# Seven block products in place of eight: Strassen's scheme in the second up projection of an fp32 encoder layer

## Chip, cores and metric

The kernel runs on one core of one Trainium2 chip. The metric is the device time of one execution in microseconds (us). A gap of 0.2% of it, 1.9 us, is about what a measurement of this kernel can tell from no change.

## What is computed

One encoder layer on 512 tokens of width 1024, all in float32, with three sub-layers: a SwiGLU feed-forward block (width 2816), a token mixer (latent attention beside causal pooling), and a second SwiGLU block. The change touches the second block:

```python
def _swiglu(h, w_in, w_out):
    g, u = jnp.split(h @ w_in, 2, axis=-1)
    return (jax.nn.silu(g) * u) @ w_out

h = x * (1.0 + scale[:, 2, None, :]) + shift[:, 2, None, :]
y = _swiglu(h, ffn2_w_in[l], ffn2_w_out[l])
x = _layernorm(ALPHA * x + 0.5 * gate[:, 2, None, :] * y, post_ln_g[l, 2], post_ln_b[l, 2])
```

## The kernel before, in words

Everything lies transposed: features on the 128 partitions, 512 tokens in the free direction. `h` is 8 tiles of 128x512 (KD = 8), the hidden layer is 22 tiles (FT = 22). Each float32 product is made of three passes in the type fp32r: an operand is split into a rounded part (`hi`) and the rest (`lo`), and `mm3` (L599 to L601) issues hi by hi, hi by lo and lo by hi. So one weight unit of 128x1024 (eight 128x128 blocks) costs 24 matmuls of 512 columns.

The weights come as a stream of units. SyncE loads a unit into one of 3 buffers `raw` (L521), ScalarE rounds it to `w_hi` (`act_hi`, L1054), VectorE subtracts and leaves `w_lo` (`dve_lo`, L1082), TensorE uses it; `w_hi` and `w_lo` have 4 slots. The order on each engine is written out by hand and held together by semaphores that count steps (`s_hi`, `s_lo`, `s_used`).

In the up stage of a feed-forward block each hidden tile t has a pair of units, gate and up. Into two PSUM banks go 24 matmuls each. Then ScalarE takes Silu of the gate bank (L1189), VectorE multiplies by the up bank (L1577), ScalarE rounds the product to `a_hi` (L1180), GpSimd leaves the rest in `a_lo` (L1926). In the down stage that follows, each of 8 output tiles takes three units (8, 8 and 6 blocks, 66 matmuls), and VectorE adds the result to the residual stream `x` (L1565). The last output tile is done in two halves of 256 tokens, 66 matmuls each of 256 columns, so that the closing LayerNorm overlaps it. During this tail only matmuls of 256 columns are to be seen.

The second block begins behind the LayerNorm of the mixer. Its first three units run on an un-normalised `h` (`opening`), the fourth and the pairs t = 2 to 21 are plain (`up`). GpSimd makes `h_lo` and scales `x` for the residual (L1920) before it comes to its first `a_lo`.

Of the kernel before, what the change touches and what calls it, by code (L numbers as in the profile page):

```python
# [22 lines left out]
P = 128  # L23
# [60 lines left out]
LAST_K = FT - 8 * (DPM - 1)  # L84

# [87 lines left out]
def source(n, wunits):  # L173
# [12 lines left out]
    return wunits[n][:, 0:unit_width(n)]  # L186
# [7 lines left out]
def unit_width(n):  # L194

    for down, end in ((F1_DOWN, MX), (F2_DOWN, UNITS)):
        if down <= n < end and (n - down) % DPM == DPM - 1:
            return LAST_K * P
    return UNIT


def build(nc, xT, wunits, ada_w, c_rows, pos_rows, cols_dram, pool_w, outT):
# [4 lines left out]
    with ExitStack() as ctx:  # L207
# [29 lines left out]
        rstd = sb("rstd", [P, TOK])
# [16 lines left out]
        ident = cols[:, C_ID:C_ID + P]  # L254

# [79 lines left out]
        def x_pair(group, half):  # L335
            return x[:, group[0]:group[1] + 1, tokens(half)]
# [17 lines left out]

        def wg(n):
# [12 lines left out]
        s_x = [sem(f"x_loaded{i}") for i in range(X_LOADS)]  # L368
        s_ada1 = [sem(f"ada_first_loaded{i}") for i in range(FIRST_RING)]
# [76 lines left out]
        s_x0 = sem("tile0_rounded")  # L446
        tile0 = {1: h_hi[:, 2, :], 2: lat[:, 2 * KD - 1, :], 3: h_hi[:, 2, :]}
# [57 lines left out]
        def _(sp):  # L505
# [197 lines left out]

# [1412 lines left out]
```

## Time and profile before

| | us |
|---|---|
| three timed runs, median (lowest to highest) | 951.12 (950.44 to 951.27) |
| profiled execution, first to last instruction (span) | 949.2 |
| TensorE busy in the span | 937.3 (99%) |
| VectorE, ScalarE, GpSimd busy | 505.9, 374.3, 267.7 |

The page gives the profiled execution by its span alone; its own time has no other figure, and the span lies 1.9 us below the median of the timed runs. PE is TensorE, PEld its weight loads, DVE VectorE, ACT ScalarE, POOL GpSimd and SP SyncE. An instruction's duration reaches from its start to the end of its last write, and on PE, DVE and ACT the next one starts before that end. So a rate is read from one start to the next, and a duration tells when a waiting engine can go on.

### The profile page before, as it was taken

How to read it: one execution, taken by the hardware profiler on the slowest of the kernel's cores; microseconds unless marked ns; L12 is line 12 of the kernel's file. 1: busy time of each engine (PE TensorE's matmuls, PEld its weight loads, DVE VectorE, ACT ScalarE, POOL GpSimd, SP SyncE). 2: the span in 40 equal slices, each digit the busy share in tenths (PEclk: the TensorE clock that was granted, in tenths of full speed). 3: DMA queues.
4: the chain of work that ended last, by engine and by line, in shares of the span. 5: the costliest groups of instructions: out<-in, count | busy, mean ns of one | idle time of the engine just before them, and what ended most of it. 6: DMA issues, size and time to landing. Idle time of an engine off the chain costs nothing.

```text
span 949.2 us, 10888 instructions
## 1 busy us (share of the span) xinstructions
PE 937.3 (99%) x4233; PEld 757.8 (80%) x4233; DVE 505.9 (53%) x714; ACT 374.3 (39%) x567; POOL 267.7 (28%) x222
## 2 busy tenths in 40 slices
PE   8999999999999999999999999999999999999997
PEld 5788888888888888788767687788888888888886
DVE  6956767545454865677666488532322322233334
ACT  6752232242222223574496457533223223221224
POOL 0021111111104512346854585611111111135125
PEclk9999999999999999999999999999999999999999
DMA  9936565656644662222421121333232232223402
GB/s 357 369 125 208 180 204 193 193 171 214 195 155 140 235 233 93 83 84 104 133 68 45 45 76 59 121 105 106 89 109 92 89 108 86 84 68 116 121 19 89
DMA packets 38563, 127.21 MB, mean 134 GB/s; under 512 B 4080, under 2 KB 6256, under 8 KB 38512
## 3 DMA queue, kind: packets, MB, share of 16 engines
q1 hardware_dynamic: 37968, 126.00, 39.5%
q8 instruction: 33, 0.54, 0.2%
q10 hardware_dynamic: 544, 0.52, 0.2%
q14 instruction: 18, 0.15, 0.0%
HBM read 123.36 MB, written 2.10 MB: 132 GB/s over the span
## 4 chain that ended last, share of the span: by engine, by line
PE 93%; DVE 3%; ACT 2%; DMA 1%; SPq 1%; issue 0%; POOL 0%; ACTq 0%; DVEq 0%
PE bank L599 29%; PE bank L601 29%; PE bank L600 29%; PE bank L957 2%; PE bank L981 1%; DMA ada_first<-ada_w 1%; PE bank L968 1%; PE bank L684 1%; PE bank L685 1%; DVE w_lo L1082 1%; PE bank L678 1%; SPq L509 0%; PE bank L874 0%; ACT act_t L1135 0%; PE bank L725 0%
## 5 line engine op out<-in xcount | busy, mean ns | idle before, releaser
L1082 DVE TENSOR_TENSOR w_lo<-raw,w_hi 128x1024 fp32r<-128x1024 f32 x152 | 204.1, 1350 | 277.7 <-ACT w_hi L1054 277.3
L599 PE MATMUL bank<-h_hi,w_hi 128*128 128x512 f32 x727 | 284.6, 391 | 0.1
L601 PE MATMUL bank<-h_hi,w_lo 128*128 128x512 f32 x727 | 283.0, 389 | 0.0
L600 PE MATMUL bank<-h_lo,w_hi 128*128 128x512 f32 x727 | 282.9, 389 | 0.0
L1054 ACT ACTIVATE w_hi<-raw 128x1024 fp32r<-128x1024 f32 x153 | 155.8, 1031 | 189.8 <-PE bank L601 188.5
L1926 POOL TENSOR_TENSOR a_lo<-act_t,a_hi 128x512 fp32r<-128x512 f32 x44 | 59.0, 1340 | 420.2 <-ACT a_hi L1180 420.2
L599 PEld LDWEIGHTS bank<-h_hi,w_hi 128*128 128x128 f32 x727 | 136.5, 188 | 29.0 <-DVE w_lo L1082 0.6
L601 PEld LDWEIGHTS bank<-h_hi,w_lo 128*128 128x128 f32 x727 | 136.4, 188 | 28.7
L600 PEld LDWEIGHTS bank<-h_lo,w_hi 128*128 128x128 f32 x727 | 136.5, 188 | 27.7
L599 PE MATMUL bank<-a_hi,w_hi 128*128 128x512 f32 (+1 forms) x374 | 141.2, 377 | 0.0
L600 PE MATMUL bank<-a_lo,w_hi 128*128 128x512 f32 (+1 forms) x374 | 140.8, 377 | 0.0
L601 PE MATMUL bank<-a_hi,w_lo 128*128 128x512 f32 (+1 forms) x374 | 140.8, 377 | 0.0
L599 PEld LDWEIGHTS bank<-a_hi,w_hi 128*128 128x128 f32 x374 | 70.4, 188 | 13.0
L600 PEld LDWEIGHTS bank<-a_lo,w_hi 128*128 128x128 f32 x374 | 70.4, 188 | 13.0
L601 PEld LDWEIGHTS bank<-a_hi,w_lo 128*128 128x128 f32 x374 | 70.4, 188 | 12.8
L1421 DVE SCALAR_TENSOR_TENSOR var<-ada_ring,c_act 128x1024 bf16<-128x1024 f32 x56 | 72.5, 1295 | 3.0 <-DMA ada_ring<-ada_w 3.0
L1180 ACT ACTIVATE a_hi<-act_t 128x512 fp32r<-128x512 f32 x44 | 27.8, 632 | 107.6 <-DVE act_t L1577 104.8
L1944 POOL TENSOR_TENSOR s_sum<-s_sum,x 128x512 f32<-128x512 f32 x17 | 27.5, 1615 | 108.0 <-DVE x L1565 105.8
L1162 ACT ACTIVATE sq<-x 128x512 f32<-128x512 f32 x20 | 12.6, 632 | 105.9 <-DVE x L1565 96.8
L1565 DVE SCALAR_TENSOR_TENSOR x<-bank,gate,x 128x512 f32<-128x512 f32 x15 | 11.2, 749 | 63.6 <-PE bank L601 58.3
L1189 ACT ACTIVATE act_t<-bank 128x512 f32<-128x512 f32 x42 | 25.1, 597 | 43.0 <-PE bank L601 43.0
L1935 POOL TENSOR_TENSOR x<-x,shift 128x512 f32<-128x512 f32 x16 | 25.9, 1656 | 56.3 <-DVE shift L1562 56.3
(304 smaller groups left out, 1046.7 us busy)
## 6 DMA issues: line engine op xcount, KB each, us to landing
raw<-wunits SPq DMA_DIRECT2D x145, 512.0 KB, 3.3
ada_ring<-ada_w SPq DMA_DIRECT2D x56, 512.0 KB, 4.4
ada_first<-ada_w SPq DMA_DIRECT2D x16, 512.0 KB, 11.4
raw<-wunits SPq DMA_DIRECT2D x16, 384.0 KB, 2.9
x<-xT SPq DMA_DIRECT2D x8, 256.0 KB, 4.9
outT<-x SPq DMA_DIRECT2D x6, 256.0 KB, 2.7
K<-k_rope SPq DMA_DIRECT2D x2, 512.0 KB, 7.8
c_act<-c_rows SPq DMA_DIRECT2D x1, 512.0 KB, 6.1
```

The lines of the kernel that those rows point to most:

```text
L599: mm(out, lh, rh, start=first, stop=False)
L600: mm(out, lh, rl, start=False, stop=False)
L601: return mm(out, ll, rh, start=False, stop=last)
L957: mm(bank[S_BANK[k % 2]][:, 0:(i + 1) * P], Q[:, hd % QRING, i * P:(i + 1) * P], K[:, hd, 0:(i + 1) * P], start=True, stop=True).then_inc( ...
L1054: nc.scalar.activation(parts(n, 0, width)[0], raw[:, slot, 0:width], ACT.Copy)\
L1082: nc.vector.tensor_tensor(lo, raw[:, slot, 0:width], hi.bitcast(F32), SUB).then_inc(s_lo, 1)
L1180: fn(a_hi[:, t - 1, :], act_t[:, (t - 1) % 2, :], ACT.Copy).then_inc(s_ah[f], 1)
L1189: fn(act_t[:, t % 2, :], bank[up_bank(f, t)][:], ACT.Silu).then_inc(s_silu[f], 1)
L1421: stt(junk, slot_ap, 1.0, c_act[:], MUL, MUL, accum_out=mod[:, t:t + 1])\
L1926: tt(a_lo[:, t, :], act_t[:, t % 2, :], a_hi[:, t, :].bitcast(F32), SUB)\
L1935: tt(x[:, m, :], x[:, m, :], shift[:], SUB).then_inc(s_xs[p], 1)
L1944: tt(s_sum[:], s_sum[:], x[:, m, :], ADD).then_inc(s_acc[p], 1)
```

## The change

For the pairs t = 5 to 21 (17 of 22) the gate and the up tile are taken together as a 2x2 scheme. The rows of blocks are gate and up, the inner dimension is halved (4 blocks of `h` each) and the tokens are halved (256 each). Plain multiplication needs eight products of 128x512 by 512x256. Winograd's form of Strassen's scheme needs seven, p1 to p7, each of 4 blocks by 3 passes, 12 matmuls of 256 columns (L984 to L986), and adds sums:

- Four sums of `h` (`t_raw`, 128x4x256 each), once, on DVE (`combine_h`), each rounded by ACT and its rest taken by DVE.
- Four sums of weight blocks for each pair. Two (up first + up second half, gate first + up first half) are made by DMA: SP loads one addend, GpSimd issues a DMA with `accum_op=ADD` that adds the other from DRAM (`add_block`). Two (`s2`, `s4`) are made by DVE, 128x512 each (`weight_sums`).
- Per pair ACT rounds 128x1024 three times and 128x512 once, and DVE takes as many rests (`rest`), where before both had two of 128x1024.
- Seven sums of results. PSUM accumulation takes two; ACT copies p1 out (`first_copy`) and DVE does five of 128x256 (`u2`, `u3`, `ub`, `ua`, `gb`). Silu is taken in two halves. One multiplication of 128x512 on DVE ends the pair.

p4 and p3 of pair t are put between p6 and p5 of pair t+1. The buffers take the room of the weight slots, in two sets; the rests are written over the raw weights. For room, `x` goes to DRAM (2 stores of 1 MB) when the stage begins, and comes back as `x2` after p4 of the last pair (4 loads of 512 KB). ACT no longer waits for `h_lo` while it makes `h` in this sub-layer, since the whole `h` is kept in `h_full`. The first five units of the down stage have waits of their own. Nothing changes before the LayerNorm of the second block.

```diff
+T0 = 5
...
+def product_order():
+    out = []
+    for t in range(T0, FT + 1):
+        if t < FT:
+            out += [("p1", t), ("p6", t)]
+        if t > T0:
+            out += [("p4", t - 1), ("p3", t - 1)]
+        if t < FT:
+            out += [("p5", t), ("p2", t), ("p7", t)]
+    return out
...
+            def load_c(t):
+                if t == T0:
+                    sp.wait_ge(s_lo, D2 - 2)
+                elif t == T0 + 1:
+                    sp.wait_ge(s_used, D2)
+                else:
+                    sp.wait_ge(s_blk, PRODUCT["p5", t - 2])
+                sp.dma_start(raw_13[in_set(t)][:, 0:BLOCK], up_unit(t)[:, 0:BLOCK]).then_inc(s_cl[in_set(t)], 16)
...
+            load_c(T0)
+            load_ab(T0)
+            load_a3(T0)
+            load_d(T0)
+            sp.wait_ge(s_res[2], KD)
+            for half in range(2):
+                k = slice(KH * half, KH * (half + 1))
+                sp.dma_start(spill[k].rearrange("t p n -> p t n"), x[:, k, :]).then_inc(s_spill, 16)
+            load_ab(T0 + 1)
+            load_c(T0 + 1)
+            load_a3(T0 + 1)
+            for t in range(T0 + 2, FT):
+                load_c(t)
+                load_ab(t)
+                load_a3(t)
+                load_d(t - 1)
+            unit(D2)
+            unit(D2 + 1)
+            load_d(FT - 1)
+            for n in range(D2 + 2, D2 + LEAD + 2):
+                unit(n)
+            sp.wait_ge(s_blk, PRODUCT["p4", FT - 1])
+            sp.wait_ge(s_spill, LOADED + 32)
+            for i in range(4):
+                sp.dma_start(x2[:, 2 * i:2 * i + 2, :], spill[2 * i:2 * i + 2].rearrange("t p n -> p t n"))\
+                    .then_inc(s_x2[i], 16)
+            for n in range(D2 + LEAD + 2, STREAM):
                 unit(n)
...
+            def product(kind, t, out, first, last):
+                hi, lo = block_parts(kind, t)
+                for kk in range(KH):
+                    cols = slice(kk * P, (kk + 1) * P)
+                    high, low = moving(kind, kk)
+                    nc.tensor.matmul(out[:, 0:HALF], hi[:, cols], high, start=first and kk == 0, stop=False, skip_group_check=True)
+                    nc.tensor.matmul(out[:, 0:HALF], hi[:, cols], low, start=False, stop=False, skip_group_check=True)
+                    done = nc.tensor.matmul(out[:, 0:HALF], lo[:, cols], high, start=False, stop=last and kk == KH - 1,
+                                            skip_group_check=True)
+                done.then_inc(s_blk, 1)
+            def block_products():
+                for t in range(T0, FT + 1):
+                    if t < FT:
+                        first, second, third = pair_banks(t)
+                        pe.wait_ge(s_blo, REST["ab", t])
+                        if t < T0 + 2:
+                            pe.wait_ge(s_prod[1], t - 1)
+                        else:
+                            pe.wait_ge(s_gs, SILU["a", t - 2])
+                        product("p1", t, first, True, True)
+                        pe.wait_ge(s_blo, REST["2", t])
+                        if t >= T0 + 2:
+                            pe.wait_ge(s_bsum, SUM["ua", t - 2])
+                        product("p6", t, second, True, True)
+                    if t > T0:
+                        _, before, gated = pair_banks(t - 1)
+                        pe.wait_ge(s_blo, REST["d4", t - 1])
+                        pe.wait_ge(s_bsum, SUM["u3", t - 1])
+                        product("p4", t - 1, before, False, True)
+                        pe.wait_ge(s_bsum, SUM["ub", t - 1])
+                        product("p3", t - 1, gated, False, True)
+                    if t < FT:
+                        pe.wait_ge(s_blo, REST["13", t])
+                        if t >= T0 + 2:
+                            pe.wait_ge(s_bsum, SUM["gb", t - 2])
+                        product("p5", t, third, True, True)
+                        pe.wait_ge(s_p1c, KD + t - T0 + 1)
+                        product("p2", t, first, False, True)
+                        pe.wait_ge(s_bsum, SUM["u2", t])
+                        product("p7", t, second, False, True)
...
+            def weight_sums(t):
+                s = in_set(t)
+                dve.wait_ge(s_acc1[s], added(t))
+                dve.wait_ge(s_ab[s], landed(t))
+                if t >= T0 + 2:
+                    dve.wait_ge(s_blk, PRODUCT["p6", t - 2])
+                sum_done(tt(raw_2[:, s, :], raw_13[s][:, 0:BLOCK], raw_ab[s][:, 0:BLOCK], ADD), "s2", t)
+                dve.wait_ge(s_bsum, SUM["s2", t])
+                if t >= T0 + 2:
+                    dve.wait_ge(s_blk, PRODUCT["p3", t - 2])
+                at = 2 * BLOCK * s
+                sum_done(tt(raw_d4[:, at:at + BLOCK], raw_2[:, s, :], raw_ab[s][:, BLOCK:2 * BLOCK], ADD), "s4", t)
+            def third_sums(t):
+                _, second, third = pair_banks(t)
+                dve.wait_ge(s_blk, PRODUCT["p7", t])
+                dve.wait_ge(s_p1c, KD + t - T0 + 1)
+                dve.wait_ge(s_prod[1], t)
+                sum_done(tt(up_sum[:, tokens(1)], p1_copy[:, in_set(t), :], second[:, 0:HALF], ADD), "u3", t)
+                dve.wait_ge(s_bsum, SUM["u3", t])
+                sum_done(tt(up_sum[:, tokens(1)], up_sum[:, tokens(1)], third[:, 0:HALF], ADD), "ub", t)
+            def second_sum(t):
+                dve.wait_ge(s_blk, PRODUCT["p6", t])
+                dve.wait_ge(s_p1c, KD + t - T0 + 1)
+                sum_done(tt(u2_sum[:, in_set(t), :], p1_copy[:, in_set(t), :], pair_banks(t)[1][:, 0:HALF], ADD), "u2", t)
...
+            def block_stage():
+                weight_sums(T0)
+                rest("ab", T0)
+                rest("2", T0)
+                product(F2, 1, T0 - 1)
+                for t in range(T0, FT + 1):
+                    if t > T0:
+                        third_sums(t - 1)
+                        rest("d4", t - 1)
+                    if t < FT:
+                        second_sum(t)
+                        rest("13", t)
+                    if t > T0:
+                        up_first(t - 1)
+                    if t + 1 < FT:
+                        weight_sums(t + 1)
+                    if t > T0:
+                        gate_second(t - 1)
+                    if t + 1 < FT:
+                        rest("ab", t + 1)
+                        rest("2", t + 1)
+                    elif t < FT:
+                        dve_lo(dve, D2)
+                        dve_lo(dve, D2 + 1)
+                    if t > T0:
+                        block_product(t - 1)
+                dve_lo(dve, D2 + 2)
...
+            def add_block(t, which):
+                s = in_set(t)
+                if which == 1:
+                    pool.wait_ge(s_cl[s], landed(t))
+                    pool.dma_start(raw_13[s][:, 0:BLOCK], wunits[F2 + 2 * t + 1][:, BLOCK:2 * BLOCK], accum_op=ADD)\
+                        .then_inc(s_acc1[s], 16)
+                else:
+                    pool.wait_ge(s_a3[s], landed(t))
+                    pool.dma_start(raw_13[s][:, BLOCK:2 * BLOCK], wunits[F2 + 2 * t + 1][:, 0:BLOCK], accum_op=ADD)\
+                        .then_inc(s_acc3[s], 16)
+            def ffn(f, p):
+                for t in range(FT if f == 0 else T0 - 2):
+                    a_split(f, t)
+                if f == 1:
+                    add_block(T0, 1)
+                    add_block(T0, 3)
+                    for t in range(T0, FT):
+                        if t + 1 < FT:
+                            add_block(t + 1, 1)
+                        a_split(f, t - 2)
+                        if t + 1 < FT:
+                            add_block(t + 1, 3)
+                    a_split(f, FT - 2)
+                    a_split(f, FT - 1)
```

**Order on VectorE.** Before, one pair of the second up stage (`w_lo` is the rest of a weight unit, `act_t` the multiplication):

```order
L1082 TENSOR_TENSOR w_lo<-raw,w_hi 128x1024 x2
L1577 TENSOR_TENSOR act_t<-act_t,bank1 128x512
L1082 TENSOR_TENSOR w_lo<-raw,w_hi 128x1024 x2
L1577 TENSOR_TENSOR act_t<-act_t,bank3 128x512
```

Now, one pair of the block stage in full (`up_sum` and `u2_sum` are sums of results, `lo_...` the rests, `raw_2` and `raw_d4` the sums s2 and s4 of the next pair's weights):

```order
L2117 TENSOR_TENSOR up_sum<-p1_copy,bank1 128x256
L2119 TENSOR_TENSOR up_sum<-up_sum,bank2 128x256
L2095 TENSOR_TENSOR lo_d4<-raw_d4,hi_d4 128x1024
L2125 TENSOR_TENSOR u2_sum<-p1_copy,bank6 128x256
L2095 TENSOR_TENSOR lo_13_0<-raw_13_0,hi_13_0 128x1024
L2130 TENSOR_TENSOR up_sum<-p1_copy,bank1 128x256
L2104 TENSOR_TENSOR raw_2<-raw_13_1,raw_ab1 128x512
L2109 TENSOR_TENSOR raw_d4<-raw_2,raw_ab1 128x512
L2136 TENSOR_TENSOR act_t<-u2_sum,bank2 128x256
L2095 TENSOR_TENSOR lo_ab1<-raw_ab1,hi_ab1 128x1024
L2095 TENSOR_TENSOR lo_2<-raw_2,hi_2 128x512
L2144 SCALAR_TENSOR_TENSOR act_t<-up_sum,act_t 128x512
```

Three instructions a pair have become twelve, and the two results that p4 waits for come first.

**Order on GpSimd**, at the beginning of the block stage; before, there stood only the rows of `a_lo`, one a pair:

```order
L2505 DMA raw_13_0<-wunits 128x512
L2509 DMA raw_13_0<-wunits 128x512
L2505 DMA raw_13_1<-wunits 128x512
L2470 TENSOR_TENSOR a_lo2<-act_t,a_hi2 128x512
L2509 DMA raw_13_1<-wunits 128x512
L2505 DMA raw_13_0<-wunits 128x512
L2470 TENSOR_TENSOR a_lo2<-act_t,a_hi2 128x512
```

Each `a_lo` now stands between two adding DMAs.

## Rows read from the trace of the kernel before

**Rows 1.** The page: busy time, TensorE's clock, the chain that ended last by engine.
```profile
PE 937.3 (99%) x4233; PEld 757.8 (80%) x4233; DVE 505.9 (53%) x714; ACT 374.3 (39%) x567; POOL 267.7 (28%) x222
PEclk9999999999999999999999999999999999999999
PE 93%; DVE 3%; ACT 2%; DMA 1%; SPq 1%; issue 0%; POOL 0%; ACTq 0%; DVEq 0%
```

**Rows 2.** Busy time by stretches of the second block: pairs 2-4, 5-21, down, tail.
```profile
core 0: us, PE busy (x) PEld busy (x) DVE busy (x) ACT busy (x) POOL busy (x), PEclk, DMA share, GB/s
598.30:630.90 32.60, 32.60 (x145) 26.95 (x144) 16.00 (x19) 12.29 (x16) 12.14 (x12) 1.00 0.43 145
630.90:815.90 185.00, 185.00 (x818) 153.18 (x817) 51.56 (x51) 54.83 (x68) 22.04 (x17) 1.00 0.29 96
815.90:920.60 104.70, 104.70 (x463) 86.69 (x462) 35.13 (x28) 23.54 (x28) 27.43 (x19) 1.00 0.26 83
```

**Rows 3.** PE in order of time: start us, duration, what; 512, then 256 columns.
```profile
894.77 0.39 PE L599 MATMUL bank<-a_hi,w_hi 128*128 128x512 f32 x1
...
920.61 0.28 PE L599 MATMUL bank<-a_hi,w_hi 128*128 128x256 f32 x1
...
928.40 0.28 PE L601 MATMUL bank<-a_hi,w_lo 128*128 128x256 f32 x1
928.52 0.28 PE L783 MATMUL bank<-h_hi,ones_d 128*128 128x256 f32 x1
```

**Rows 4.** DVE in order of time, tail: sums of 256 columns, and starts behind PE.
```profile
928.72 0.48 DVE L1483 SCALAR_TENSOR_TENSOR x<-bank,gate,x 128x256 f32<-128x256 f32 x1 [3.72 <-PE bank L601]
931.84 0.43 DVE L1487 SCALAR_TENSOR_TENSOR bank<-bank,tmp 128x256 f32<-128x256 f32 x1 [2.63 <-PE bank L795]
932.18 1.28 DVE L1491 TENSOR_TENSOR x<-x,bank 128x512 f32<-128x512 f32 x2
933.38 0.42 DVE L1494 TENSOR_TENSOR bank<-bank,y 128x256 f32<-128x256 f32 x1
933.83 0.43 DVE L1496 SCALAR_TENSOR_TENSOR bank<-bank,y 128x256 f32<-128x256 f32 x1
```

**Rows 5.** DVE in order of time, one pair of the second up stage.
```profile
632.04 1.23 DVE L1082 TENSOR_TENSOR w_lo<-raw,w_hi 128x1024 fp32r<-128x1024 f32 x1 [3.79 <-ACT w_hi L1054]
633.18 0.68 DVE L1577 TENSOR_TENSOR act_t<-act_t,bank 128x512 f32<-128x512 f32 x1
637.90 1.23 DVE L1082 TENSOR_TENSOR w_lo<-raw,w_hi 128x1024 fp32r<-128x1024 f32 x1 [4.04 <-ACT w_hi L1054]
```

**Rows 6.** ACT by groups, shapes apart: rounding, copies of 256 columns, rounding `a_hi`.
```profile
L1054 ACT ACTIVATE w_hi<-raw 128x1024 fp32r<-128x1024 f32 x137 | 143.5, 1054 | 181.1 <-PE bank L601 179.8 <-DMA raw<-wunits 1.3
L1107 ACT ACTIVATE tmp<-bank 128x256 f32<-128x256 f32 x2 | 0.8, 384 | 1.0 <-PE bank L789 1.0
L1180 ACT ACTIVATE a_hi<-act_t 128x512 fp32r<-128x512 f32 x18 | 11.4, 632 | 35.2 <-DVE act_t L1577 32.5 <-DVE act_t L1573 2.7
```

**Rows 7.** POOL and DVE in order of time, behind the last pair: the two overlap.
```profile
817.35 1.29 POOL L1926 TENSOR_TENSOR a_lo<-act_t,a_hi 128x512 fp32r<-128x512 f32 x1 [7.37 <-ACT a_hi L1180]
...
818.25 1.47 DVE L1082 TENSOR_TENSOR w_lo<-raw,w_hi 128x1024 fp32r<-128x1024 f32 x1 [1.65 <-ACT w_hi L1054]
```

**Rows 8.** DMA issues: size each, median us from issue to landing.
```profile
raw<-wunits SPq DMA_DIRECT2D x145, 512.0 KB, 3.3
K<-k_rope SPq DMA_DIRECT2D x2, 512.0 KB, 7.8
poolw<-pool_w SPq DMA_DIRECT2D x1, 256.0 KB, 2.9
```

**Rows 9.** PEld's longest idle piece early in the program, and a clock row around it.
```profile
23.49 0.30 PEld L678 LDWEIGHTS bank<-h_lo,w_hi 128*128 128x128 f32 x2 [1.55 <-DVE h_lo L1719]
...
20.00:30.00 10.00, 7.52 (x32) 4.74 (x32) 9.93 (x18) 9.89 (x15) 0.00 (x0) 1.00 1.03 418
```

More of the change, by code:

```diff
@@ L194, in unit_width @@
 def unit_width(n):
-    for down, end in ((F1_DOWN, MX), (F2_DOWN, UNITS)):
+    for down, end in ((F1_DOWN, MX), (D2, STREAM)):
         if down <= n < end and (n - down) % DPM == DPM - 1:
@@ L446, in build, with added, landed @@
         s_x0 = sem("tile0_rounded")
+        s_gs, s_p1c = s_xna, s_tfree
+        s_acc1 = [sem(f"first_sum_added{i}") for i in range(2)]
+        s_acc3 = [sem(f"third_sum_added{i}") for i in range(2)]
+        s_ab, s_cl, s_a3 = s_ada1[4:6], s_ada1[6:8], s_ada1[8:10]
+        s_d, s_spill, s_x2 = s_x[0], s_x[1], s_x[2:6]
+        LOADED = 16
+        s_blk, s_bhi, s_blo, s_bsum = s_tp, s_fc, s_tok, s_xk
+        PRODUCT = counts(product_order(), KD)
+        ROUNDED = counts(rounding_order(), KD)
+        REST = counts(rest_order(), 2 * QB)
+        SUM = counts(sum_order(), QB)
+        SILU = counts(silu_order(), 2 * QB)
+        def added(t):
+            return 16 * ((t - T0) // 2 + 1)
+        def landed(t):
+            return LOADED + 16 * ((t - T0) // 2 + 1)
         tile0 = {1: h_hi[:, 2, :], 2: lat[:, 2 * KD - 1, :], 3: h_hi[:, 2, :]}
@@ L837, in down, with ffn @@
                     down_tile(base, per, p, rhs, k_last, m, ready)
-            def ffn(base, f, p, a_hi, a_lo):
+            def ffn(base, down_base, f, p):
                 if f == 0:
@@ L1176, in up, with silu_whole @@
+            def silu_whole(base, f, t):
+                act.wait_ge(s_used, base + 2 * t + 1)
+                if t >= 2:
+                    act.wait_ge(s_al[f], t - 1)
+                fn(act_t[:, t % 2, :], bank[up_bank(f, t)][:], ACT.Silu).then_inc(s_silu[f], 1)
+            def up(base, f):
+                for t in range(FT + 1 if f == 0 else T0 - 1):
                     if t < FT and split_next(base, 2 * t) is not None and (f == 0 or t >= 2):
@@ new lines, in rest @@
+            def rest(kind, t):
+                s = in_set(t)
+                dve.wait_ge(s_bhi, ROUNDED[kind, t])
+                if kind in ("ab", "2"):
+                    dve.wait_ge(s_bsum, SUM["s4", t])
+                if kind == "T":
+                    out, whole, hi = t_lo[:, t], t_raw[:, t], t_hi[:, t]
+                elif kind == "ab":
+                    out, whole, hi = lo_ab[s][:], raw_ab[s][:], hi_ab[s][:]
+                elif kind == "2":
+                    out, whole, hi = lo_2[:, s, :], raw_2[:, s, :], hi_2[:, s, :]
+                elif kind == "13":
+                    out, whole, hi = lo_13[s][:], raw_13[s][:], hi_13[s][:]
+                else:
+                    out, whole, hi = lo_d4[:, d4_columns(t)], raw_d4[:, d4_columns(t)], hi_d4[:]
+                tt(out, whole, hi.bitcast(F32), SUB).then_inc(s_blo, 1)
@@ L1642, in ffn @@
                     product(base, f, t)
-                for t in range(early, FT + 1):
+                for t in range(early, FT + 1 if f == 0 else T0 - 1):
                     for j in range(2):
-                        if t < FT and (f == 0 or 2 * t + j >= LEAD):
+                        if t < FT and (f == 0 or LEAD <= 2 * t + j < 2 * T0 - LEAD):
                             dve_lo(dve, split_next(base, 2 * t + j))
@@ L1652, in ffn @@
                         rope_chunk(t - ROPE_FIRST)
+                if f == 1:
+                    combine_h()
+                    for j in range(4):
+                        rest("T", j)
+                    product(base, f, T0 - 2)
+                    block_stage()
                 if f == 0:
```

454 lines of the change are left out of this document (365 added, 89 removed).

## Prediction, made before the changed kernel was run

> **What bounds the kernel now.** I read the page first. PE is busy for 99% of the span and makes 93% of the chain that ended last, with its clock granted in full in all 40 slices [rows 1]. So whatever takes time out of PE takes it out of the kernel, as long as the others keep up. The table by stretches says whether they would: during pairs 5 to 21, PE works 185.0 of 185.0 us, DVE 51.6, ACT 54.8 and POOL 22.0 [rows 2]. All helpers have room, and the DMA engines are busy 0.29 of the time.
>
> Then the rate of PE, start to start. From 894.77 to 920.61 there are 114 matmuls of 512 columns, 0.2267 us each. From 920.61 to 928.52 there are 66 of 256 columns, 0.1199 us each [rows 3]. Half the columns cost more than half the time, 0.1199 against 0.1133, so seven products of eight do not give an eighth. The four matmuls from 928.52 on, behind a wait of their own, come without a gap, so a wait that is already met costs nothing.
>
> **The gain.** A pair takes 48 x 0.2267 = 10.88 us before, and 7 x 12 = 84 matmuls, 84 x 0.1199 = 10.07 us, after. That is 0.81 us a pair (0.813 unrounded) and **13.8 us** for 17 pairs. This is all the change can give. One product takes 12 x 0.1199 = 1.44 us.
>
> **Do the helpers fit into 10.07 us?** By starts, DVE needs 1.14 us for 128x1024 [rows 5], 0.60 for 128x512 (two in 1.20, from 932.18 to 933.38) and 0.34 for 128x256 (931.84 to 932.18); an instruction that waits for the one ahead comes 0.45 behind it [rows 4]. A pair has three of 1024, four of 512 and five of 256 columns: 3.42 + 2.40 + 1.70, and 0.2 for the two that wait, 7.7 us. ACT has three roundings of 1024 at 1.05, two of 512 at 0.63 and three pieces of 256 at 0.38 [rows 6]: 5.6 us. POOL has one `a_lo` of 1.29 [rows 7] and two DMA issues that no row shows. So nobody is the bound by its sum. What counts is when each result comes.
>
> Call the start of pair t on PE T. p1 and p6 run to T + 2.88, p4 and p3 of the pair before to T + 5.75, then p5, p2, p7 to T + 10.07.
>
> - **p4 behind p7.** p4 waits for u3 and for the rest d4, which DVE can begin only when p7 of its pair is done. DVE starts 0.20 us behind the next matmul (928.52, 928.72), u3 takes 0.45, ub 0.34 [rows 4], the rest 1.23 to its last write [rows 5]: 2.22, say 2.27 with the way back to PE. The cover is p1 and p6, 2.88 us, so 0.6 is spare. But POOL's `a_lo` falls here: ACT rounds d4 and then `a_hi` right behind p2 and p7. The row at 818.25 overlaps an `a_lo` by 0.39 us and takes 1.47 in place of 1.23 [rows 5, 7], a loss of 0.62 us for each us of overlap. A whole `a_lo` costs up to 0.8, 0.2 over the spare. I take 0.1 for each of 16 pairs, the middle of 0 and 0.2: **+1.6** (0 to 3.2).
> - **The adding DMA.** Let L be its time from POOL's turn to landing. Its other addend is loaded when p5 of the pair before last is done, 2.88 before T, and lands 0.2 + 2.9 later [rows 8], T + 0.2. DVE asks for the sum for s2 at T + 3.08 + 0.34 (u2) + 1.14 (rest 13) + 0.34 (ua) = T + 4.9. So L up to 4.7 is free. Behind it stand s2, s4, gb, two rests and the multiplication, 4.0 us. They may end 0.2 + 0.6 after the next T, so L up to 6.6 only eats room. Past that each us costs PE half a us a pair, because a late p4 also moves p5 and with it the next load.
> - **What L is.** No row shows an adding DMA. From below, a plain load of 256 KB lands in 2.9 us. From above, the slowest kind near it, SBUF as source, takes 7.8 for 512 KB. 512 KB of plain load take 3.3 [rows 8], so a second read of 256 KB is worth some 0.4. That and about 1.2 us for POOL to issue, an estimate from the length of its one compute instruction, give L = 4.5. It is nearest to the plain row, as the transfer has the same shape and size.
> - **Beginning of the stage.** In pair 5 nothing stands between p6 and p5. PE idles 0.20 + 0.34 (u2) + 1.23 (rest 13) + 0.05 = 1.8 us. Then the first operand of pair 6: load at T5 + 0.2, landed + 2.9, added + 4.5, then s2 and s4 1.3, the rest ab 1.3: T5 + 10.2, where PE is ready at 2.88 + 1.8 + 4.31 = 9.0. So 1.2 more: **+3.0** (1.8 with L = 2.9, 6.3 with L = 7.8). The sums of `h` and their rests are 8 DVE instructions of 1.14, some 9.5 us, behind the multiplication of pair 2, where DVE is busy 16.0 of 32.6 us [rows 2]. With them the rests of pair 5 end about 1 us before PE asks.
> - **End of the stage.** Behind p7 of pair 21 no p1 and p6 cover the chain to p4. PE idles for all of it: **+2.6** (2.3 to 3.1 with an `a_lo` in it).
> - **Hidden.** Storing `x` (2 MB) goes to the queue while no load is urgent. The reload and the down units behind it (2 MB, four times 3.3 us at the slowest) end within 14 us of p4, and the first residual comes 18 us after it (p3 and the 66 matmuls of an output tile, 15.0 us). If that cover went, each us of lateness would stall PE only from the third output tile. DMA traffic goes from 0.5 MB a load twice in 10.9 us to 1.8 MB in 10.1, less than half of the rate that the row at 20 to 30 us shows, 418 GB/s [rows 9]. POOL has `a_lo` later than before, but the down stage asks for the last ones 13 us into it.
>
> **Sum.** -13.8 + 1.6 + 3.0 + 2.6 = -6.6 us. It is made against the profiled execution (span 949.2 us); nothing outside the stage changes, so I set it against the median of 951.1: **944.5 us**. With the ends of this case, -13.8 + 0 + 1.8 + 2.3 gives 941.4, and L = 6 with full overlap, -13.8 + 3.2 + 4.5 + 3.1, gives 948.1.
>
> The Trainium skill, page "DMA: Bandwidth & Descriptors", section on the anatomy of a DMA on the GpSimd path, fits 2.0 us and the bytes over 436 GB/s to one such DMA; by it 256 KB is 2.6 us, the beginning costs 1.8 in place of 3.0, and the result would be 943.3. It says nothing of adding.
>
> **Rivals.**
>
> 1. *The adding DMA is late, and the kernel is slower.* At L = 7.8 the beginning costs 6.3, each of 16 pairs about 0.8 (half of 1.2, and some overlap), the end 2.9: -13.8 + 6.3 + 12.8 + 2.9 = +8.2, **959.3 us**. It turns to a loss from L = 7.0. For it: an addition reads two sources and writes over one of them, two of them a pair stand in one queue, and POOL waits for `a_hi` between them. Against it: all plain rows of this size are at 2.9.
> 2. *The port between DVE and POOL.* If POOL's making of two DMAs a pair hinders DVE as `a_lo` does, 0.6 us for each us, p4 is late by about 0.5 in each pair: -13.8 + 8.0 + 3.2 + 2.9 = +0.3, **951.4 us**, no change. For it: DVE has 12 instructions a pair, and the rest ahead of p4 has 0.6 spare. Against: no row shows that issuing costs DVE anything.
> 3. *The clock.* The longest idle piece of PE's loads early in the program is 1.55 us, and the stretch around it has the clock at 1.00 in spite of 2.5 us idle in 10 [rows 9]. My gaps are 1.8, 1.2 and 2.6. If the last one, longer than any seen, brought the clock to its lower level over one pair's worth of matmuls, these would take twice 10.07 us: +10.1, **954.6 us**. The Trainium skill, page "TensorE: Matmul & The Clock Gate", Part 1, has the clock fall to 1.2 GHz when the engine idles; by that rule this rival holds, by the row it does not.
> 4. *It does not do what it says.* The listing has 84 matmuls of 256 columns a pair, so this gets nothing.
>
> **Chances.** Forecast 0.70 (941.4 to 948.1); rival 1 0.14; rival 2 0.11; rival 3 0.05. A difference of 0.2%, 1.9 us, is about what can be told from none. Faster by more: 0.70, and 0.03 of the weaker forms of rivals 1 and 2. Within it: 0.07, mostly rival 2. Slower: 0.20. The range takes in the forecast case and rival 2, 941.2 to 952.0; what it leaves out is most of rivals 1 and 3.
>
> **What would show it.** The start-to-start time inside a product is 0.120 us. PE idles three times at the edges of the stage: 1.8 ahead of the first p5, about 1.2 ahead of pair 6, 2.6 ahead of the last p4. Inside, the period of a pair is 10.07 to 10.3 us, and any idle time stands ahead of p4, ended by the rest d4. The adding DMA lands in 4 to 5 us. I am wrong if the period is over 10.4, if the idle time is ended by s2 or its successors (rival 1), if DVE's 128x1024 mean is well over 1.4 us in the stage (rival 2), or if the clock row drops (rival 3).

## The result, and the profile after it

The changed kernel takes **957.84 us** (median of 4 runs, 957.49 to 957.96), the kernel before 951.14 (950.44 to 951.27) in the same comparison: a ratio of 1.0072, 95% interval 1.0058 to 1.0086. It is slower by 6.7 us. The forecast was 944.5, the range ended at 952.0, and "slower" had 0.20.

The page of the kernel after, beside [rows 1]:

```profile
PE 929.1 (97%) x4845; PEld 779.5 (82%) x4845; DVE 618.8 (65%) x875; ACT 412.4 (43%) x639; POOL 298.6 (31%) x256
PEclk9999999999999999999999999999999999999999
PE 88%; DVE 6%; DMA 4%; issue 1%; SPq 1%; ACT 1%; ACTq 0%; DVEq 0%
```

PE's share of the chain fell from 93% to 88%, DVE's doubled. The clock's row in 40 slices shows nothing. The same three stretches as in [rows 2], cut where the first p1 and the first matmul of the down stage stand:

```profile
598.30:630.39 32.09, 32.09 (x143) 26.55 (x142) 25.48 (x28) 15.67 (x20) 12.77 (x13) 1.00 0.58 188
630.39:822.49 192.10, 176.77 (x1429) 173.52 (x1428) 153.25 (x201) 88.68 (x134) 51.99 (x50) 0.99 0.68 166
822.49:927.00 104.51, 104.51 (x462) 86.54 (x462) 36.66 (x30) 24.70 (x30) 27.56 (x19) 1.00 0.31 104
```

All of the loss is in the middle row, 192.1 us where there were 185.0. Of the 1428 matmuls at 0.1199 us, 171.2 us is the work; so the stage has lost 20.9 us, with 13.8 us to give. Its waits on PE (who waited, for whom, us in total, times, longest):

```profile
PE bank L984 <- DVE lo_d L2095: 12.3, 13, 2.9
PE bank L984 <- DVE lo L2095: 1.6, 1, 1.6
PE bank L984 <- DVE lo_ab L2095: 1.3, 1, 1.3
```

`lo_d` is the rest d4, which p4 waits for, `lo` of 128x1024 the rest 13 (for p5), `lo_ab` the rest for p1. L984 is the first matmul in each group of three. From one matmul's start to the next, less 0.1199, the 20.9 us are:

| where | forecast | found |
|---|---|---|
| start of the stage: ahead of the first p5 (1.8) and of pair 6 (1.5), and the matmul behind each (0.1) | 3.0 | 3.5 |
| inside: ahead of p4 of 13 of 16 pairs, 0.24 to 1.3 each, and 0.1 behind each | 1.6 | 12.9 |
| end: ahead of the last p4 | 2.6 | 3.2 |
| matmuls at the lower clock behind that gap | 0 | 1.3 |

The edges are right, and one line is wrong by a factor of eight. One pair in order of time, DVE, then POOL, then PE:

```profile
706.68 0.42 DVE L2117 TENSOR_TENSOR up_sum<-p_copy,bank 128x256 f32<-128x256 f32 x1 [0.89 <-PE bank L986]
707.13 0.42 DVE L2119 TENSOR_TENSOR up_sum<-up_sum,bank 128x256 f32<-128x256 f32 x1
707.47 3.14 DVE L2095 TENSOR_TENSOR lo_d<-raw_d,hi_d 128x1024 fp32r<-128x1024 f32 x1
710.53 0.41 DVE L2125 TENSOR_TENSOR u_sum<-p_copy,bank 128x256 f32<-128x256 f32 x1
...
707.33 0.86 POOL L2505 DMA_DIRECT2D raw<-wunits  x1 [6.47 <-DMA raw<-wunits]
707.89 1.63 POOL L2470 TENSOR_TENSOR a_lo<-act_t,a_hi 128x512 fp32r<-128x512 f32 x1
...
710.66 0.38 PE L984 MATMUL bank<-t_hi,hi_d 128*128 128x256 f32 x1 [1.15 <-DVE lo_d L2095]
```

The rest takes 3.14 us, not 1.23 [rows 5]. `a_lo` ends at 709.52, the rest at 710.61: 1.09 later, about a whole undisturbed one. It did not go slower beside `a_lo`; it stood until `a_lo` was over. In the three pairs without a gap the rest begins 0.6 to 0.7 us ahead of `a_lo` (and just ahead of POOL's DMA issue), and takes 1.22; here `a_lo` is the longer one:

```profile
752.21 1.22 DVE L2095 TENSOR_TENSOR lo_d<-raw_d,hi_d 128x1024 fp32r<-128x1024 f32 x1
...
752.25 0.86 POOL L2505 DMA_DIRECT2D raw<-wunits  x1 [5.40 <-DMA raw<-wunits]
752.81 1.77 POOL L2470 TENSOR_TENSOR a_lo<-act_t,a_hi 128x512 fp32r<-128x512 f32 x1
```

DVE's groups in the stage (busy, mean ns, idle before) show that it is this rest that is hit:

```profile
L2095 DVE TENSOR_TENSOR lo_d<-raw_d,hi_d 128x1024 fp32r<-128x1024 f32 x17 | 40.9, 2408 | 0.0
L2095 DVE TENSOR_TENSOR lo<-raw,hi 128x1024 fp32r<-128x1024 f32 x17 | 20.7, 1220 | 0.0
L2104 DVE TENSOR_TENSOR raw<-raw,raw_ab 128x512 f32<-128x512 f32 x16 | 11.0, 689 | 7.6 <-DMA raw<-wunits 7.6
```

The last row holds the other suspect: DVE waits 7.6 us for the added block. And the DMA issues (size, median us to landing), beside [rows 8]:

```profile
raw<-wunits SPq DMA_DIRECT2D x34, 256.0 KB, 3.4
raw<-wunits POOLq DMA_DIRECT2D x34, 256.0 KB, 4.9
```

L, the time from the issue of the adding DMA to its landing, is 4.9 us where 4.5 was taken. The clock, behind the longest gap, PE in order of time:

```profile
818.17 0.39 PE L984 MATMUL bank<-t_hi,hi_d 128*128 128x256 f32 x1 [2.92 <-DVE lo_d L2095]
...
819.23 0.28 PE L986 MATMUL bank<-t_hi,lo_d 128*128 128x256 f32 x1
819.35 0.36 PE L984 MATMUL bank<-t_hi,hi_d 128*128 128x256 f32 x1
819.50 0.42 PE L985 MATMUL bank<-t_lo,hi_d 128*128 128x256 f32 x1
...
822.28 0.41 PE L986 MATMUL bank<-h_hi,lo_d 128*128 128x256 f32 x1
```

From 819.50 to 822.28 there are 13 steps of 0.214 us, the lower level of the clock (1.2 GHz), where the ones ahead are 0.12 apart (2.4 GHz).

**Theories.** A: POOL's `a_lo` holds up the rest d4 for the whole of its length, and p4 waits. B (rival 1 of the prediction): the adding DMA is late, and DVE, late with the sums, comes late to all else. C (rival 2): POOL's making of the DMAs does it. D: DVE has too much to do in this order whatever POOL does.

### The profile page after: what moved, and what is told of

It reads as the page before. It is cut to its first block, busy times and chain, and to the rows that moved or that the text cites. A ratio compares the mean times of both kernels' runs of the same rounds, so it can differ in the third digit from the quotient of the medians.

```text
span 956.2 us, 12629 instructions
## 1 busy us (share of the span) xinstructions
PE 929.1 (97%) x4845; PEld 779.5 (82%) x4845; DVE 618.8 (65%) x875; ACT 412.4 (43%) x639; POOL 298.6 (31%) x256
## 4 chain that ended last, share of the span: by engine, by line
PE 88%; DVE 6%; DMA 4%; issue 1%; SPq 1%; ACT 1%; ACTq 0%; DVEq 0%
PE bank L873 23%; PE bank L875 23%; PE bank L874 22%; PE bank L984 5%; PE bank L986 4%; PE bank L985 4%; DVE lo_d L2095 4%; DMA raw<-wunits 3%; PE bank L1276 2%; PE bank L1300 1%; DMA ada_first<-ada_w 1%; PE bank L1287 1%; DVE up_sum L2117 1%; PE bank L1043 1%; DVE up_sum L2119 1%
## 5 line engine op out<-in xcount | busy, mean ns | idle before, releaser
L1403 DVE TENSOR_TENSOR w_lo<-raw,w_hi 128x1024 fp32r<-128x1024 f32 (+1 forms) x117 | 161.4, 1389 | 134.0 <-ACT w_hi L1375 133.6
L873 PE MATMUL bank<-h_hi,w_hi 128*128 128x512 f32 x455 | 178.6, 393 | 0.0
L875 PE MATMUL bank<-h_hi,w_lo 128*128 128x512 f32 x455 | 177.2, 389 | 0.0
L874 PE MATMUL bank<-h_lo,w_hi 128*128 128x512 f32 x455 | 177.1, 389 | 0.0
L1375 ACT ACTIVATE w_hi<-raw 128x1024 fp32r<-128x1024 f32 (+1 forms) x118 | 118.8, 1023 | 121.2 <-PE bank L875 118.4
L875 PEld LDWEIGHTS bank<-h_hi,w_lo 128*128 128x128 f32 x455 | 85.4, 188 | 18.0
L873 PEld LDWEIGHTS bank<-h_hi,w_hi 128*128 128x128 f32 x455 | 85.4, 188 | 17.9 <-issue 0.5
L984 PE MATMUL bank<-t_hi,hi 128*128 128x256 f32 x204 | 57.8, 284 | 1.6 <-DVE lo L2095 1.6
L1483 ACT ACTIVATE sq<-x 128x512 f32<-128x512 f32 x20 | 12.6, 632 | 105.5 <-DVE x L1986 96.4
L985 PE MATMUL bank<-t_lo,hi 128*128 128x256 f32 x204 | 57.7, 283 | 0.0
L986 PE MATMUL bank<-t_hi,lo 128*128 128x256 f32 x204 | 57.7, 283 | 0.0
## 6 DMA issues: line engine op xcount, KB each, us to landing
ada_first<-ada_w SPq DMA_DIRECT2D x16, 512.0 KB, 11.6
```

Of the source, the lines that this page charges most:

```text
L873: mm(out, lh, rh, start=first, stop=False)
L874: mm(out, lh, rl, start=False, stop=False)
L875: return mm(out, ll, rh, start=False, stop=last)
L984: nc.tensor.matmul(out[:, 0:HALF], hi[:, cols], high, start=first and kk == 0, stop=False, skip_group_check=True)
L985: nc.tensor.matmul(out[:, 0:HALF], hi[:, cols], low, start=False, stop=False, skip_group_check=True)
L986: done = nc.tensor.matmul(out[:, 0:HALF], lo[:, cols], high, start=False, stop=last and kk == KH - 1, skip_group_check=True)
```

## Experiments

The kernel before, on the chips of these runs, took 950.67 to 950.82. Each ratio is against it.

### 1. The adding DMAs left out

```diff
-                dve.wait_ge(s_acc1[s], added(t))
+                dve.wait_ge(s_cl[s], landed(t))
...
-                        if t + 1 < FT:
-                            add_block(t + 1, 1)
                         a_split(f, t - 2)
-                        if t + 1 < FT:
-                            add_block(t + 1, 3)
```

The two additions of pair 5 and ACT's waits for the additions are left out as well.

> The adding DMAs are left out, so two of the four weight sums lack an addend; everything else stays, a_lo too, which POOL now starts as soon as a_hi is there. Late-add theory: the loads are in time at once, PE's idle time goes, 940 to 944. Turns theory: a_lo begins 0.4 us earlier, still ahead of the rest d4 and for 1.3 us; the rest d4 ends about 1.1 us behind it, some 0.6 us earlier than with the DMA issue in front, so PE idles 0 to 0.4 us a pair and the time is 945 to 950; the rest d4 takes 1.8 to 2.3 us.

Measured: 949.5 us (10 runs, 947.25 to 951.33), ratio 0.9985 (0.9975 to 0.9994). DVE and POOL in order of time:

```profile
704.09 2.07 DVE L2095 TENSOR_TENSOR lo_d<-raw_d,hi_d 128x1024 fp32r<-128x1024 f32 x1
...
703.78 1.30 POOL L2470 TENSOR_TENSOR a_lo<-act_t,a_hi 128x512 fp32r<-128x512 f32 x1 [9.12 <-ACT a_hi L1498]
```

`a_lo` ends at 705.08, the rest at 706.16: 1.08 later again, with no DMA made by POOL at all. In 15 of the 16 pairs 0.24 us stand ahead of p4 and 0.1 behind its first matmul, a period of 10.42. So B is not the cause, and A stands without C. But 8.3 us of 957.8 did go. Ahead of pair 6, where the sum waited for the added block, the gap of 1.5 us is gone. Inside the stage most of what went is POOL's DMA issue, which no longer stands ahead of `a_lo` and moves its end back: there the adding DMA costs more by its place in POOL's order than by its landing (experiment 5).

### 2. POOL's pair of instructions put behind the sum ub

```diff
                     for t in range(T0, FT):
+                        if t > T0:
+                            pool.wait_ge(s_bsum, SUM["ub", t - 1])
                         if t + 1 < FT:
                             add_block(t + 1, 1)
```

> GpSimd waits for ub of the pair before ahead of its first adding DMA, so that the rest d4 on DVE has begun when POOL starts. Turns theory (DVE and POOL take the shared path by whole instructions, the first one in goes first; 13.0 us of idle PE ahead of p4 in 14 of the pairs come from rests d4 of 2.5 to 3.1 us that began behind POOL's DMA issue or a_lo): all rests d4 take 1.22 us, PE's idle time inside the stage falls from 13.0 to under 1 us, the gap ahead of the last p4 from 3.1 to 2.3, and the clock stays: 958 falls by 14 to 15 us, to 943 to 945. Late-add theory (rival 1): the adding DMA starts 0.7 us later, so the time rises or stays at 958 to 962.

Measured: 945.21 us (942.59 to 947.14), ratio 0.9938 (0.9919 to 0.9958). The instructions are the same, only POOL's start moves, and the rest d4 is 1220 ns in all 17 pairs. Now `a_lo` meets the next rest of 128x1024 on DVE, the rest 13 that p5 waits for (mean 1704 ns), which has more room. (The same wait stands ahead of the last two `a_lo`.) The idle time inside the stage is one gap of 0.82; the rest of the 10.4 us lost stands at the edges, 3.56 ahead of the first p5 and 2.26 ahead of the last p4, each followed by matmuls at the lower clock (3.6 us of the 10.4, slow first matmuls behind the gaps included). The gap of 3.56 was not expected, and it is `a_lo` again. The rest 13 of pair 5 takes 2.97 us:

```profile
633.14 2.97 DVE L2095 TENSOR_TENSOR lo<-raw,hi 128x1024 fp32r<-128x1024 f32 x1
```

The new wait does not touch this pair, and in the kernel after the same rest took 1.22, at 633.80. POOL's instructions came 0.4 us earlier here against DVE's. So which of the two comes first at the beginning of the stage is not fixed by the program's order.

### 3. `a_lo` made by DVE

```diff
                     if t < FT:
                         second_sum(t)
                         rest("13", t)
+                    low_on_dve(t - 2)
                     if t > T0:
                         up_first(t - 1)
```

For pairs 3 to 21 DVE makes `a_lo`; POOL keeps only the adding DMAs.

> The a_lo of pairs 3 to 21 is made on DVE (between the rest 13 and ua), GpSimd only issues adding DMAs. If a_lo alone is what holds DVE up, rests d4 take 1.22 us and the time falls to 943 to 946 (DVE has 0.6 us more a pair, inside its spare time). If the issuing of the adding DMA (0.87 us on POOL, right at the rest d4) holds DVE up as well, the rests d4 take up to 2.0 us and PE still idles some 0 to 0.3 us a pair: 945 to 949. Late-add theory: no change, 957 to 959.

Measured: 944.36 us (942.89 to 944.69), ratio 0.9928 (0.9913 to 0.9943). DVE has 19 instructions more, and the kernel is 13.5 us faster than with them on POOL: D falls. On C, DVE and POOL in order of time:

```profile
705.34 0.69 DVE L2150 TENSOR_TENSOR a_lo<-act_t,a_hi 128x512 fp32r<-128x512 f32 x1
...
704.76 0.86 POOL L2517 DMA_DIRECT2D raw<-wunits  x1 [1.67 <-DMA raw<-wunits]
```

A DVE instruction with two inputs in SBUF overlaps a DMA issue and takes its usual 0.69, and the rest d4, which begins inside an issue in several pairs, has a mean of 1219 ns. C falls as well.

### 4. The rest d4 ahead of the sums u3 and ub

```diff
-                        third_sums(t - 1)
                         rest("d4", t - 1)
+                        third_sums(t - 1)
```

> DVE takes the rest d4 ahead of u3 and ub, which frees it from waiting for p7: it starts about 0.1 us into the pair, 0.7 us ahead of POOL's DMA issue, and u3 and ub read PSUM and one tile of SBUF. Turns theory: rests d4 1.22 us, no idle time ahead of p4 inside the stage, the gap ahead of the last p4 falls from 3.1 to about 1.4 us and with it the drop of the clock goes: 958 falls by 16 us, to 941 to 943. Late-add theory: 956 to 958.

Measured: **942.72 us** (941.82 to 942.93), ratio 0.9912 (0.9897 to 0.9927). Two lines exchanged turn a loss of 6.7 us into a gain of 8. The rest no longer stands behind p7, and DVE is through with it before `a_lo` begins:

```profile
701.54 1.23 DVE L2095 TENSOR_TENSOR lo_d<-raw_d,hi_d 128x1024 fp32r<-128x1024 f32 x1 [0.38 <-ACT hi_d L1535]
702.68 0.41 DVE L2117 TENSOR_TENSOR up_sum<-p_copy,bank 128x256 f32<-128x256 f32 x1
703.13 0.42 DVE L2119 TENSOR_TENSOR up_sum<-up_sum,bank 128x256 f32<-128x256 f32 x1
...
702.97 1.61 POOL L2470 TENSOR_TENSOR a_lo<-act_t,a_hi 128x512 fp32r<-128x512 f32 x1
```

The ub at 703.13 lies inside `a_lo` and takes 0.42 as ever; one of its two inputs is in PSUM. The idle time left is 1.81 and 1.74 at the start, 0.54 once, and 1.83 at the end: 6.4 us with the matmuls behind them, and none of it at the lower clock.

### 5. Experiment 4 without the adding DMAs

The diffs of experiments 1 and 4 together.

> As e3 (rest d4 first), with the adding DMAs left out, so that two of the four weight sums lack an addend. If an adding DMA that lands in 4.9 us costs PE nothing once DVE is not held up, only the start of pair 6 gets earlier (its sum waits for the add there): e3 less 1 to 2 us, 940.5 to 942. If late or slow adds still cost something inside the stage: under 940.

Measured: 940.95 us (940.51 to 942.48), ratio 0.9896 (0.9881 to 0.9912). With DVE free, the adding DMAs are worth about 1.8 us in all, issues and landings together (the runs of the two kernels overlap, 941.82 to 942.93 and 940.51 to 942.48). The gap ahead of pair 6 (1.74) and the one of 0.54 are gone; the first gap of the stage is longer, 2.15, and has matmuls at the lower clock behind it.

### 6. `a_lo` ahead of the adding DMA on POOL

```diff
-                        if t + 1 < FT:
-                            add_block(t + 1, 1)
                         a_split(f, t - 2)
+                        if t + 1 < FT:
+                            add_block(t + 1, 1)
                         if t + 1 < FT:
                             add_block(t + 1, 3)
```

> The changed kernel with a_lo ahead of the first adding DMA on POOL in place of behind it; the adding DMA is still there and starts about 0.5 us later than in the changed kernel. Turns theory: a_lo begins as a_hi is done, as in e4, so the rests d4 take 2.0 us and the pairs 10.4 us as there: 948 to 951. If the adding DMA itself (its traffic, its landing) took PE's time: 956 to 960, as in the changed kernel or later.

Measured: 956.88 us (954.96 to 959.56), ratio 1.0058 (1.0041 to 1.0075). As a time this is a miss of theory A, by 5.9 us, and lies in the range of the other one. The rest d4 came down as expected, to 2.08 us where 1.29 of `a_lo` is in front:

```profile
710.25 2.08 DVE L2095 TENSOR_TENSOR lo_d<-raw_d,hi_d 128x1024 fp32r<-128x1024 f32 x1
...
709.95 1.29 POOL L2470 TENSOR_TENSOR a_lo<-act_t,a_hi 128x512 fp32r<-128x512 f32 x1 [7.41 <-ACT a_hi L1498]
711.19 0.87 POOL L2505 DMA_DIRECT2D raw<-wunits  x1
```

But the time did not. DVE's waits from 645 to 800 us:

```profile
DVE raw L2104 <- DMA raw<-wunits: 18.0, 12, 2.7
```

The DMA is issued 1.2 us later behind `a_lo`, and later still in three pairs in which the rest goes first and `a_lo` itself takes 2.1 to 2.3 us:

```profile
688.00 1.22 DVE L2095 TENSOR_TENSOR lo_d<-raw_d,hi_d 128x1024 fp32r<-128x1024 f32 x1
688.07 2.29 POOL L2470 TENSOR_TENSOR a_lo<-act_t,a_hi 128x512 fp32r<-128x512 f32 x1 [6.92 <-ACT a_hi L1498]
```

DVE asks for its block up to 2.7 us too early, then a gap of 0.5 stands ahead of p1 and one of 1.35 ahead of p4. The gaps inside the stage sum to 9.3 us, where experiment 1, without the DMA, has 3.6. So B is real as a mechanism: its margin in this kernel is about 1 us, and one exchange on POOL uses it up. The 3.67 us ahead of the first p5, with 25 matmuls at the lower clock behind them, are not B: the rest 13 of pair 5 takes 3.08 there beside an `a_lo`, as in experiment 2.

### 7. Experiment 4, with the end of the stage mended

In the last pair ACT rounds d4 ahead of Silu.

```diff
-                    silu_first(t)
-                    round_block("d4", t)
+                    if t == FT - 1:
+                        round_block("d4", t)
+                    silu_first(t)
+                    if t < FT - 1:
+                        round_block("d4", t)
```

> As e3 (rest d4 ahead of u3 and ub), and in the last pair ACT rounds d4 ahead of the first Silu half, so that the last rest d4 does not wait for p2. The gap ahead of the last p4 in e3 is 1.8 us; left of it is the way from p7 over u3, 0.2 + 0.45 us. Expected: 1.1 us less than e3, 941.6, the other gaps as there.

Measured: 943.38 us (940.68 to 944.87), ratio 0.9919 (0.9902 to 0.9937). A miss as a time. In the profiled execution (942.83) the last gap shrank from 1.83 to 0.79 as it should, but one load of the second addend was late and made a gap of 1.50 at 766.26. The four runs spread over 4.2 us, so 1 us can't be told by them.

### 8. Experiment 4, with the start mended

The first rest 13 goes ahead of the multiplication of pair 4, and `raw_13` and `raw_ab` of the second set exchange places, so that the addend of pair 6, and not its plain pair, gets the room that is free first.

```diff
                 rest("2", T0)
+                rest("13", T0)
                 product(F2, 1, T0 - 1)
...
-            load_ab(T0 + 1)
             load_c(T0 + 1)
             load_a3(T0 + 1)
+            load_ab(T0 + 1)
```

> As e3, with the beginning of the stage mended: the rest 13 of pair 5 goes ahead of the multiplication of pair 4, and the first addend of pair 6 gets the place in SBUF that is free one unit (5.4 us) earlier. In e3 PE idles 1.8 us ahead of the first p5 and 1.7 ahead of pair 6, and 0.2 in slower single matmuls. If both are only lateness of these two results: 3.7 us down to 0 to 1.2, so 939.0 to 940.2. If the first gap only moves to pair 6, because the load of gate 6 or its sums are late in any case: 941 to 943.

Measured: 939.68 us (939.52 to 941.34), ratio 0.9888 (0.9873 to 0.9902). The gap of 1.8 ahead of the first p5 is gone, that ahead of pair 6 is 1.16 in place of 1.74, the end has 1.83 still.

### 9. Experiments 4, 7 and 8 together

Their three diffs, nothing else.

> Rest d4 first, mended end (e5) and mended beginning (e6) together: PE's idle time in the stage falls from 20.9 us in the changed kernel to under 2.5. 957.8 - 20.9 + 2 = 938.9; expected 938 to 940, which is 11 to 13 us under the kernel before and close to the 13.8 us that the count of matmuls allows.

Measured: **939.23 us** (938.18 to 940.28), ratio 0.9879 (0.9864 to 0.9894). This beats both kernels, the one before by 11.6 us. Its waits on PE in the stage:

```profile
PE bank L984 <- DVE up_sum L2120: 0.6, 1, 0.6
PE bank L984 <- DVE lo_ab L2098: 0.5, 1, 0.5
```

The stage takes 173.0 us, 1.8 over its 171.2 of work. The gain of the seven products is there almost in full.

### 10. Experiment 9, with POOL behind the sum ub as in experiment 2

The diff of experiment 2 on top of experiment 9.

> e7 and the wait of e1 together: POOL starts its DMA and a_lo only when ub is done. In e7 no rest d4 is held up any more, so the turns theory gives no gain; the adding DMA starts later by 0.9 us, and it has little room: 939 to 941, the same as e7 or up to 1.5 us slower, with DVE waiting for the add ahead of s2.

Measured: 947.7 us (945.96 to 948.5), ratio 0.9966 (0.9954 to 0.9979). A miss by 8 us, and a second case of the same mechanism. Here ub comes behind the rest d4, so POOL starts right ahead of the next rest, 13 (`lo`):

```profile
705.84 2.54 DVE L2098 TENSOR_TENSOR lo<-raw,hi 128x1024 fp32r<-128x1024 f32 x1
...
705.65 1.62 POOL L2475 TENSOR_TENSOR a_lo<-act_t,a_hi 128x512 fp32r<-128x512 f32 x1
...
708.42 0.39 PE L984 MATMUL bank<-t_hi,hi 128*128 128x256 f32 x1
```

`a_lo` ends at 707.27, the rest 1.11 later at 708.38, and p5 begins at 708.42, 0.25 us late. The mean of this rest is 2725 ns over the stage, against 1704 in experiment 2 and 1344 in experiment 9, and 0.24 to 0.79 us stand ahead of p5 in 15 pairs. In experiment 2 the rest d4 stood between ub and this rest, and took up `a_lo`'s time.

## Why the prediction was wrong

**The step that failed is the one headed "p4 behind p7"**: "a loss of 0.62 us for each us of overlap. A whole `a_lo` costs up to 0.8, 0.2 over the spare", the term of +1.6 (0 to 3.2). It measured 12.9. The row it came from said more than I took from it [rows 7]: `a_lo` ends at 817.35 + 1.29 = 818.64, and the `w_lo` beside it at 818.25 + 1.47 = 819.72, 1.08 later. With the 3.14, 2.07, 2.08 and 2.54 us of the rows above, the end is 1.08 to 1.11 behind `a_lo` each time. I had read two durations and called their difference a rate; the two ends show a wait. The same trace of the kernel before had a longer overlap, in the down stage, that tells the two apart:

```profile
863.40 2.01 POOL L1946 TENSOR_TENSOR q_sum<-q_sum,sq 128x512 f32<-128x512 f32 x1
864.18 2.31 DVE L1082 TENSOR_TENSOR w_lo<-raw,w_hi 128x1024 fp32r<-128x1024 f32 x1
```

By the rate of 0.62 an overlap of 1.23 us makes 1.23 into 2.0; by the wait it ends 1.08 behind 865.41, at 866.49, and so it does. As a wait, a rest that meets `a_lo` at its start takes 1.29 + 1.09 = 2.4 us, against the 1.23 + 0.6 that the cover allowed: 0.5 to 0.6 a pair in place of the 0.1 taken or the 0.2 at most. The remainder up to 1.3 comes from POOL's DMA issue of 0.86 ahead of `a_lo`, which makes the rest up to 3.1 long. No row of the kernel before has such an issue, but the prediction counts 1.2 us for it in L and none for it here. What the rows could not give is which pairs are hit; 13 of 16 were.

I had also taken POOL's order without its coupling: the DMA issue and `a_lo` behind it start at about the time that DVE comes to the rest d4, and the issue moves `a_lo` back by its own length. Without the issue (experiment 1) a pair loses 0.34.

The Trainium skill, page "SBUF — State Buffer", section "Who interferes with whom", says that a DVE instruction with two SBUF inputs contends with a GpSimd one that reads SBUF, that one with at most one SBUF input does not, and, of DVE's 2-port modes, that whoever issues first has the shared ports for the whole instruction. The traces agree on the first two (the rests of 2.1 to 3.1 us, the ub of 0.42), and show the wait for the whole instruction for a plain subtraction too.

**The other steps.**

- *The gain.* Right: 0.1199 from start to start in every product, and experiment 9 gives 11.6 of the 13.8 us.
- *The helpers by their sums.* Right, and no help: DVE is busy 153.3 of 192.1 us, waiting in `lo_d` included. Experiment 3 gave it more work, and the kernel was faster.
- *The adding DMA.* L of 4.9 for the 4.5 taken; with DVE free the adding DMAs cost some 1.8 us, most of it at pair 6 (experiments 4 and 5). But the free L of 4.7 was right as a bound as well, so this kernel stood at its edge: with an issue 1.2 us later and more (experiment 6) the gaps inside the stage are 5.7 us more than without the DMA (experiment 1).
- *Beginning and end.* Right: 1.8, 1.5 and 3.1 for 1.8, 1.2 and 2.6; the 3.1 has the `a_lo` in it that was its upper end. That the first was 1.8 was in part luck: in experiments 2 and 6 an `a_lo` falls there too, and it is 3.56 and 3.67.
- *Hidden.* The store and reload of `x` show no wait, and the down stage takes 104.5 us where it took 104.7 [rows 2].
- *Rival 1.* Its time (959.3) is near the result, its cause is not: without the DMA the idle time ahead of p4 is still there (experiment 1), and with the rest d4 out of the way the landing costs 1.8 us (experiment 5), where the rival had 12.8 inside the stage alone. A number that fits says nothing about the mechanism.
- *Rival 2.* The right place, and a p4 late by 0.5 a pair was near the 0.8 found, but the wrong actor: the compute instruction on POOL, not the DMA issue (experiment 3), which only moves the end of `a_lo` back (experiment 1).
- *Rival 3.* It happened, over 14 matmuls of this stage in place of 84: 1.3 us, not 10.1. I gave it one size, a whole pair, with no row for that.

**What would have been seen from the list of signs:** the start-to-start time, the three edge gaps, "any idle time stands ahead of p4, ended by the rest d4", and the landing all came true; the period came out over 10.4 (10.9 us, p4 at 654.83 to p4 at 807.79 in 14 pairs), and the 128x1024 mean of `lo_d` is 2408 ns. They name the right place at once.

## What to carry to other kernels

When two instructions overlap in a trace and one is longer than usual, compare their ends before the difference of their durations: an end that follows the other's by one undisturbed length is a wait, and its price is what is left of the other instruction when the first one comes, up to the whole of it, and more if something stands ahead of it on its own engine. When DVE subtracts from SBUF on a path with little spare, look at what GpSimd starts just ahead of it, its DMA issues included; to exchange two instructions on DVE was worth 15 us here. And a fix by order is local to that order: POOL's wait for ub gave 12.6 us alone, and cost 8.5 us on top of the better order.

## What was not expected of the hardware

- **Turns between DVE and GpSimd.** A subtraction on DVE with both inputs in SBUF waited for the whole of `a_lo` and ended 1.08 to 1.11 us behind it. It goes both ways: where the subtraction comes first, it takes its 1.22 and `a_lo` ends 1.14 us behind it (688.00 and 688.07, experiment 6, with no issue in front). Where a DMA issue stands ahead of `a_lo`, the rests of 128x1024 in all these traces part by how far ahead of the recorded start of `a_lo` they begin. Up to 0.42 us ahead they are held (707.47 against 707.89), from 0.49 us on they are not, even if the issue has begun, as here in experiment 4:

```profile
682.15 0.86 POOL L2505 DMA_DIRECT2D raw<-wunits  x1 [5.90 <-DMA raw<-wunits]
682.38 1.23 DVE L2095 TENSOR_TENSOR lo_d<-raw_d,hi_d 128x1024 fp32r<-128x1024 f32 x1 [0.89 <-ACT hi_d L1535]
682.95 1.81 POOL L2470 TENSOR_TENSOR a_lo<-act_t,a_hi 128x512 fp32r<-128x512 f32 x1
```

An issue alone holds nothing (experiment 3). POOL's starts are rough in the records, and the 1.62 recorded behind an issue is likely the 1.29 of an undisturbed `a_lo` and a rest of the issue; why an `a_lo` behind an issue has the turn before its work can have begun stays open.
- **The clock.** Behind all gaps from 2.15 us on the matmuls came at the lower level (1.2 GHz), 0.21 us apart, at once or up to 12 matmuls later: 2.15 in experiments 1 and 5, 2.26 in 2 and 3, 3.08 in 1, 6 and the kernel after, 3.56 in 2, 3.67 in 6. Behind those of up to 1.83 (after, experiments 4, 5 and 8) they kept 0.12. In the kernel after the page's clock row has a 9 in every slice; it is the spacing that shows the fall. The Trainium skill, page "TensorE: Matmul & The Clock Gate", Part 1, has the clock fall to 1.2 GHz when the engine idles; the longer gaps agree, the shorter ones show no fall.
- **An adding DMA** of 256 KB lands in 4.9 us by the median from POOL's issue, where a plain one of the same kernel has 3.4; POOL is held 0.86 us by the issue.
- **Spread.** The kernels with the scheme vary by 0.5 to 4.6 us from run to run, the kernel before by 0.5 to 0.9. In one profile a late load is seen as a gap (experiment 7), at the edges of the stage the lower clock comes or not, and the rest 13 of pair 5 is held by an `a_lo` in some kernels and not in others (experiments 2 and 6). That these make the whole spread was not shown, as each kernel has one trace.
